# Two heads' attention scores on halves of the array's rows, and an input load split in four, in a two-layer streaming encoder step

## What is computed

```
fox:  p = softmax(q k^T / 8 + cum_q - cum_k);   o = p v          (cum: running sum of log forget gates)
sb:   z = q k^T / 8;  log_beta = logsigmoid(z);  log_rest = logsigmoid(-z)
      a = exp(log_beta + (sum of log_rest over the later keys));   o = a v
```

## Time and profile before

| | |
|---|---|
| median of 3 runs | 1479.09 us (1476.92 to 1482.16) |
| profiled execution, own time | 1475.89 us |
| profiled execution, span | 1473.8 us |
| PE busy | 1202.0 us (82%) |
| DVE, ACT, POOL busy | 674.3, 430.6, 228.4 us |
| mean granted clock of PE | 0.925 of full |

### The profile page before, as it was taken

One profiled execution on the slowest core, in us unless ns is written; L12 is line 12 of the kernel. 1 busy time (PEld: TensorE's weight loads), 2 busy tenths in 40 slices (PEclk: granted clock), 3 DMA queues, 4 the chain that ended last, 5 costly groups with the idle time before them and its releaser, 6 DMA issues. The chain is left out here.

```text
span 1473.8 us, 24136 instructions
## 1 busy us (share of the span) xinstructions
PE 1202.0 (82%) x8148; PEld 830.6 (56%) x8148; DVE 674.3 (46%) x1859; ACT 430.6 (29%) x981; POOL 228.4 (15%) x366
## 2 busy tenths in 40 slices
PE   6887898997894998787769699999989499878770
PEld 4766677775773555344346466777567355444430
DVE  4455654444654353222263356555665535322226
ACT  3555664444310211011122244444530121111111
POOL 1111112222112232221110000000001223211123
PEclk9999999999995999889979899999999599999995
DMA  4212123411619999999670120000041999999975
GB/s 165 75 61 74 30 96 104 162 53 46 255 75 380 361 367 371 386 371 382 267 251 1 45 119 16 15 30 15 2 162 45 391 368 363 357 375 390 388 286 193
DMA packets 61381, 290.80 MB, mean 197 GB/s; under 512 B 12688, under 2 KB 23120, under 8 KB 44256
## 3 DMA queue, kind: packets, MB, share of 16 engines
q1 hardware_dynamic: 49408, 265.90, 48.8%
q0 software_dynamic: 10560, 18.90, 4.0%
q10 hardware_dynamic: 1312, 4.72, 0.8%
HBM read 275.91 MB, written 29.29 MB: 207 GB/s over the span
## 5 line engine op out<-in xcount | busy, mean ns | idle before, releaser
L1756 PE MATMUL psum<-w_gu,moe_xgT 128*64 128x256 f32 x1968 | 260.7, 409 | 70.3 <-DMA w_gu<-in_w_gate_up 49.8
L1756 PEld LDWEIGHTS psum<-w_gu,moe_xgT 128*64 128x64 f32 x1968 | 153.5, 146 | 161.3 <-issue 116.5
L199 PE MATMUL psum<-x_hi,ab_w_hi 128*128 128x288 f32 x384 | 126.6, 330 | 7.4 <-ACT ab_k_tok L723 4.7
L1804 ACT ACTIVATE moe_silu<-psum 64x256 f32<-64x256 f32 x64 | 24.2, 378 | 338.2 <-PE psum L1756 293.9
L1829 DVE COPY moe_xgT<-psum 128x512 f32<-128x512 f32 x64 | 44.3, 692 | 168.0 <-PE psum L1746 167.1
L201 PE MATMUL psum<-x_hi,ab_w_lo 128*128 128x288 f32 x384 | 116.1, 302 | 0.0
L200 PE MATMUL psum<-x_lo,ab_w_hi 128*128 128x288 f32 x384 | 116.0, 302 | 0.0
L1703 POOL DMA_INDIRECT y_d<-mix,moe_slots x60 | 55.5, 925 | 363.0 <-DVE mix L1842 352.2
L1773 PE MATMUL psum<-w_dn,moe_hidT 128*64 128x512 f32 x352 | 85.1, 604 | 2.2 <-issue 2.2
L199 PEld LDWEIGHTS psum<-x_hi,ab_w_hi 128*128 128x128 f32 x384 | 75.1, 196 | 13.6 <-issue 11.8
L1837 DVE COPY moe_hidT<-psum 128x128 f32<-128x128 f32 x64 | 18.7, 292 | 140.1 <-PE psum L1764 138.6
(11 more groups left out here) (305 smaller groups left out, 2162.3 us busy)
## 6 DMA issues: line engine op xcount, KB each, us to landing
w_gu<-in_w_gate_up SPq DMA_DIRECT2D x54, 2048.0 KB, 35.1
w_dn<-in_w_down SPq DMA_DIRECT2D x44, 1024.0 KB, 36.2
xT<-in_w_down SPq DMA_DIRECT2D x20, 1024.0 KB, 40.2
w_gu<-in_w_gate_up SPq DMA_DIRECT2D x10, 1536.0 KB, 39.7
w_gu<-in_w_out SPq DMA_DIRECT2D x4, 2048.0 KB, 8.7
combine_ys<-y_d SPq DMA_DIRECT2D x16, 512.0 KB, 8.5
xT<-in_w_gate_up SPq DMA_DIRECT2D x10, 512.0 KB, 42.4
xT<-cum_d SPq DMA_DIRECT2D x8, 544.0 KB, 7.1
```

What stands on the lines that cost most here:

```text
L199: nc.tensor.matmul(dst, r32(ah), r32(bh), start=first, stop=False)
L1756: last = nc.tensor.matmul(gu(s)[h * CB:(h + 1) * CB, 0:EH], xgT[:, s, j, :], gate_up_tile(k.w_gu[n], j)[:, h * EH:(h + 1) * EH], start=(j ...
```

## The change

The gates' matrix gets a semaphore of its own, x comes in four parts, `b_f` and `logf_past` are issued behind the first q weights, and `products` waits for the matrix and the parts of x alone. In the first layer `scores` takes only a head's own 64 partitions of queries and keys. For row tiles 0 to 3 of both kinds of pair a new function `both_scores` issues the two heads' matmuls one after the other, head 0 on array rows 0 to 63 and head 1 on rows 64 to 127, after one common wait. The sb pairs' lead on PE becomes 4, so their units 8 and 9 are placed as in the fox pairs: after `turn(4)` and after `turn(5)` with `values`, ahead of kt and v0. ACT's, DVE's and POOL's lists stay (their own sb lead is still 3), as does the filling of the queries' unused halves with zeros.

```diff
-        self.xt_in = [sem("xt_in0"), sem("xt_in1")]
+        self.xt_in = [sem(f"xt_in{n}") for n in range(4)]
+        self.wf_in = sem("wf_in")
...
-        sp.dma_start(self.wf, k.w_f).then_inc(self.f_in, 16)
-        for b in range(2):
-            sp.dma_start(k.xT[:, 4 * b:4 * b + 4, 0:T], k.x_t[:, 4 * b:4 * b + 4, :]).then_inc(self.xt_in[b], 16)
-        sp.dma_start(self.bf, k.b_f).then_inc(self.f_in, 16)
-        sp.dma_start(self.logf[:, SEQ:NEW_AT], k.logf_past).then_inc(self.f_in, 16)
+        sp.dma_start(self.wf, k.w_f).then_inc(self.wf_in, 16)
+        for b in range(4):
+            sp.dma_start(k.xT[:, 2 * b:2 * b + 2, 0:T], k.x_t[:, 2 * b:2 * b + 2, :]).then_inc(self.xt_in[b], 16)
         for n in range(3):
             sp.dma_start(k.wp[n][:].rearrange("p j n -> p (j n)"), k.w_ab[n]).then_inc(k.wp_in[n], 16)
+            if n == 0:
+                sp.dma_start(self.bf, k.b_f).then_inc(self.f_in, 16)
+                sp.dma_start(self.logf[:, SEQ:NEW_AT], k.logf_past).then_inc(self.f_in, 16)
...
-        pe.wait_ge(self.f_in, 48)
+        pe.wait_ge(self.wf_in, 16)
         for j in range(J):
-            if j % 4 == 0:
-                pe.wait_ge(self.xt_in[j // 4], 16)
+            if j % 2 == 0:
+                pe.wait_ge(self.xt_in[j // 2], 16)
...
-                    q = qh[par][h][0:QW, t * P:t * P + rows] if mla else qh[par][h][:, t * P:t * P + rows]
-                    key = kh[par][h][0:QW, lo:lo + width] if mla else kh[par][h][:, lo:lo + width]
+                    at = slice(0, QW) if mla else slice(h * HD, (h + 1) * HD)
+                    q = qh[par][h][at, t * P:t * P + rows]
+                    key = kh[par][h][at, lo:lo + width]
...
+                def both_scores(p, par, t):
+
+                    n = UNITS * p + 2 * t
+                    if t == 0:
+                        hold(pe, passed, (s["proj_act"], STEPS * (p + 1)), (s["proj_dve"], STEPS * (p + 1)), (s[f"kp_in{par}"], of_parity(16, p, par)))
+                    elif t >= 2:
+                        hold(pe, passed, (s["scored"], n - 2))
+                    for h in range(2):
+                        _, _, rows, lo, width = unit_of(2 * t + h)
+                        at = slice(h * HD, (h + 1) * HD)
+                        nc.tensor.matmul(slot(2 * t + h)[0:rows, 0:width], qh[par][h][at, t * P:t * P + rows], kT[par][at, lo:lo + width],
+                                         start=True, stop=True).then_inc(s["scores_ready"], 1)
...
-                    lead = SB_LEAD if kind == "sb" else LEAD
-                    for u in range(lead):
-                        scores(p, par, u, lead)
+                    lead = LEAD
+                    if kind == "mla":
+                        for u in range(lead):
+                            scores(p, par, u, lead)
+                    else:
+                        both_scores(p, par, 0)
+                        both_scores(p, par, 1)
                     projections(-1)
                     for u in range(UNITS):
                         turn(p, u, kind)
                         if u >= 3 and u % 2:
                             values(p, par, u // 2 - 1)
-                        if u + lead < UNITS:
+                        if kind != "mla" and u + lead < UNITS - 2:
+                            if u % 2 == 0:
+                                both_scores(p, par, u // 2 + 2)
+                        elif u + lead < UNITS:
                             scores(p, par, u + lead, lead)
                         projections(u)
```

More of the change, by code:

```diff
@@ L320, in split_x_hi @@
         for j in range(J):
-            if j % 4 == 0:
-                act.wait_ge(self.xt_in[j // 4], 16)
+            if j % 2 == 0:
+                act.wait_ge(self.xt_in[j // 2], 16)
             split_hi(self.nc, self.k.x_hi[:, j, :], self.k.xT[:, j, 0:T]).then_inc(self.x_hi_done, 1)
@@ L328, in logs @@
         act.wait_ge(self.z_ready, 1)
-        act.wait_ge(self.f_in, 48)
+        act.wait_ge(self.f_in, 32)
         steps.then(self.nc.scalar.activation(self.t_abs, self.z, ACT.Abs, bias=self.bf))
@@ L343, in sums @@
         logf, low, t_ln, cum, ones = self.logf, self.low, self.t_ln, self.cum, self.ones
-        dve.wait_ge(self.f_in, 48)
+        dve.wait_ge(self.f_in, 32)
         dve.wait_ge(self.act_step, 1)
```

## The result

The changed kernel takes 1513.57 us (median of 4 runs, 1511.21 to 1513.67) against 1479.29: ratio 1.0226, 95% interval 1.0203 to 1.0249. It is 34.3 us slower, as forecast in direction; 1499 was too low and the top of the range, 1511, was missed. In the profiled execution the first layer's pairs end at 404.9 us instead of 372.3, and the unedited rest adds another 5.

The account below looks back on a forecast made before the run. PE was taken to bound the fox pairs, the chain through ACT, DVE and POOL to hold up sb pairs. Start -4.7, sb +26.0, fox -1.1 gave +20.2: 1475.9 to 1496.1, with the median 3.2 above, 1499; range 1486 to 1511.

Parts of the forecast that it names:

- The start: Gates' products before the first projection: PE begins at 5.4 instead of 10.12, first projection at 16.2 instead of 20.92; -4.7 us.
- What both heads save: Scores of tiles 0 to 3: both heads' matmuls run at once, 2.15 us saved a pair, less 0.20 a mode change.
- Strict order of matmuls: Reason offered for heads running in line: only head 0's second record and head 1's first overlap, half the saving lost; 1503.
- Sb pairs: the mechanism: Unit 9, now ahead of v0, waits for unit 7's L920, delaying v0 and turn(6): +4.5 us a pair, bounds 3.2 and 5.2.
- The clock: Behind unit 9's 6.4 us wait in sb pairs PE comes back slow: +2.0 us a pair, bounds 0 and 4.4.
- the clock stays up: Rival: no slow clock behind unit 9's wait in the sb pairs; 12.2 instead of 20.2, 1491 us; chance 0.18.
- The places of the bursts: Tiles 2 and 3 among the projections: fox pairs lose 0.65 to waiting; sb pairs' chain +0.5 from turn(1) on.
- Fox pairs: 2.15 saved less 1.15 for changes and 0.65 back as waiting: 0.35 us gained a pair in three pairs, -1.1.
- The last pair: Last fox pair: has no projections and waits on DVE anyway, so no gain was counted there.
- The small stall: Rival: unit 9's stall in sb pairs is only about 1.5 us a pair and cancels against the start; 1479; chance 0.04.
- the covered wait: Rival: unit 9's wait in sb pairs is covered and PE sets all pairs; 1472 us; chance 0.05.
- The heads in line: Rival: heads run one after the other on row halves, in part (1503 us) or wholly (1508); chance 0.12.

Follow-up runs that it names:

- the first experiment: Changed kernel with the sb pairs' units 8 and 9 back at their old places, bursts and new start kept: 1486.06 us, ratio 1.0027.

## Why the prediction was wrong in size

By the medians of kernel after kernel the steps are: start -4.4, bursts at the change's places +9.7 (1485.03 - 1475.36), unit 9's stall +15.5, its clock +13.0; such steps add up to the whole by construction. Forecast: -4.7, -1.1, +18.0, +8.0; sum +20.2.

The profiled executions divide it otherwise. The four sb pairs together took 181.5 us before, 184.7 with unit 9 alone back, 206.5 with the wait filled and 216.6 after: bursts +3.2, stall +21.8, clock +10.0, where 26.0 was forecast for all. From before to after that is +35.1 of 37.7 in the span; the first scores come 3.5 earlier, fox pairs give 0.0, the last pair +1.0, and the unedited stages +5.1. The medians give the bursts more and the stall less. A likely reason is that the kernel with unit 9 back stands between them, and that its last pair of 34.6 is in neither the kernel before nor the one after; in how many of its executions it is so long is not known.

- **The start** was right. That 5.4, 16.2 and the quarter of x at 5.3 came out at 5.91, 15.83 and 5.80 says the row could be shifted as it stood.
- **What both heads save** was right: full overlap, 0.20 for a change back. The Trainium skill, "TensorEngine Tiling (Array Packing)", section Key Properties, has a change of tiling drain the engine; the 0.20 agrees with a cost, and no run separates its draining from the weight load. Strict order of matmuls would have left head 1's second record of tile 2 alone, 0.98 with no change counted; the trace has 0.85 with it. That order is what the Trainium skill states, "TensorE: Matmul & The Clock Gate", section The mechanism; for these records the trace does not agree.
- **Sb pairs: the mechanism** was right: unit 9 waits for unit 7's L943, and v0 and `turn(6)` wait behind it. In the first pair unit 9 starts 31.8 us after the pair's first scores, where 31.4 was forecast, in the others at 33.9, 32.7 and 33.9; in the second, q1 and tile 3's burst had already run at half clock. The stall cost 3.9 a pair by the medians and 5.5 by the profiled pairs, where 4.5 was taken with bounds of 3.2 and 5.2, so its size is open.
- **The clock** is a failed step: "half of a slow stretch is lost ... I take 2.0". The filled wait shows 3.3 a pair by the medians and 2.5 by the profiled pairs, inside the bounds of 0 and 4.4. I took the short stretch that followed one wait of 2.5; behind the waits of 6.3 and 5.7 the two windows above last 6.8, with PE at work for 4.5 and 5.0 of it. This makes +5.0 or +2.0. The rival "the clock stays up" is refuted.
- **The places of the bursts**, tile 2's above all, are the other: "the 0.65 comes back as waiting", netted to a gain of 0.35 in a fox pair, and "+0.5 on the whole chain" in an sb pair, which I counted as swallowed by unit 9's wait. Both terms came out at an unbroken clock, but they were priced as waits that cost their own length alone. With unit 9 back, the bursts cost 9.7 by the medians where -1.1 stood (+3.2 in the profiled sb pairs), and moving tile 2's alone takes off 16.1 (1486.06 to 1470.00; with tile 3's burst later, 5.6, which is not clear of noise). The profiled executions of these two kernels differ by 11.6: 6.2 in the first layer, of which the rows show 1.1 an sb pair at full clock, and the rest in stages that were not edited (1104.3 and 1099.0 us, at mean granted clocks of 0.90 and 0.91). From run to run the time goes with the granted clock: in the first experiment from 1472.66 us at 0.919 to 1491.17 at 0.906. The median of the runs' clocks is 0.910 there, 0.917 with tile 2's burst later and 0.92 with the start alone, so part of what the places cost goes with a lower clock; which wait brings it down is not shown.
- **Fox pairs** came out at 0.0 where 0.35 was forecast: the wait ahead of `turn(2)` took 0.65 as said, and one of 0.32 to 0.34 ahead of `turn(0)` came on top.
- **The last pair** was taken to wait on DVE anyway; it lost 1.0, and 3.2 with later bursts.
- **The unedited stages** were put at nothing; they took 5.1 more, at a mean clock of 0.90 against 0.91. Over all the profiled executions here they took 1098.7 to 1108.6, so that the change did this is not shown.

The small stall and the covered wait (1479, 1472) are refuted by the rows of unit 9. The heads in line (1503 to 1508) come nearer the time than my number, but by the wrong cause. What stays open is how the loss divides between stall and bursts, and the part of the 16.1 that the rows don't place; the runs of those kernels spread over 6 to 20 us.

## What to carry to other kernels

When a queue's order is changed, ask for each moved instruction what its hold waits for at the new place, and price what is queued behind it; the engine time that it saves says little. A wait of PE of several us (5.7 and 6.3 here) costs its own length and then the clock: price both from the longest stretch of half clock that a like wait was followed by. Work taken from PE is worth something only where PE sets the end, and a burst earns most where it runs inside a wait: with units 8 and 9 at their old places, the same matmuls one projection step later turned a ratio of 1.003 into 0.992, part of it with the higher clock.

## What the hardware showed

- Two float32 matmuls on halves of the array's rows ran wholly side by side: four records of 384 columns in the time of two.
- Useless matmuls in a wait kept the granted clock at 1.00 behind it in three of four pairs, where an idle PE came back at 0.50 for 6.8 us in all four; the same wait without them cost 13 us by the medians.
- Executions of one kernel differ with the mean granted clock: with both bursts later, twelve runs go from 1468.27 us at 0.921 to 1480.41 at 0.905.
- A half clock of 34 us appeared in the last pair of the kernel with unit 9 back, longer than any in the first layer's attention of the kernel before (10.2), though PE was busy for 24.6 of it; the last pair took 34.6. Last pairs of 34.6 and 35.2 in two other kernels (bursts in fox pairs only at the change's places; tile 3's later) stand beside it. Nothing here tells why. The window of that stretch, and one as long in an unedited stage of the kernel before, where PE was busy for 16.8 of 37.5:
```profile
348.30:382.40 34.10, 24.62 (x113) 14.32 (x114) 17.72 (x50) 17.28 (x43) 7.55 (x17) 0.50 0.33 125
```
```profile
442.80:480.30 37.50, 16.80 (x91) 13.91 (x93) 15.34 (x97) 3.28 (x13) 7.80 (x8) 0.50 1.01 376
```
